# Second half's down products behind the first half's in-projection, and its taps on VectorE

## The reference

```python
# first block, feed-forward
h = rms_norm(x, norm_ffn_g)
gp = dwconv_centered(h @ w_ffn_gate, ffn_conv_w, ffn_conv_b)     # 3 taps along S, 2816 channels
x = x + (silu(gp) * (h @ w_ffn_up)) @ w_ffn_down
# second block, conformer mixer
h = rms_norm_2(x, mix_norm)
a, g = jnp.split(h @ w_in + b_in, 2, axis=-1)
h = a * jax.nn.sigmoid(g)
h = conv(h, conv_w)            # depthwise along S, 31 taps, causal: position s sees s-30 to s
h = silu(layer_norm(h + conv_b, ln_g, ln_b))
x = x + (h @ w_out + b_out)
# second block, MLP
x = x + jnp.square(relu(rms_norm_2(x, mlp_norm) @ w1)) @ w2
```

## Time and profile before

| | |
|---|---|
| median of 3 runs | 3266.32 us (3264.25 to 3274.74) |
| profiled execution | 3276.46 us, its span 3274.6 us |
| mean granted clock of TensorE | 0.982 of full |
| feed-forward, first to last product | about 1454 to 2176 us |
| from there to the first up product | 2176 to 2516.7 us |
| bytes moved | 288.8 MB |

### The profile page before, as it was taken

The page is one execution under the profiler, slowest core; times in us unless marked ns, Lnnn a source line. Parts: engine busy times, 40 slices in busy tenths (PEclk is TensorE's granted clock), DMA queues, the critical chain, the costliest instruction groups (busy, mean ns, idle before and its releaser), DMA issues.

```text
span 3274.6 us, 54823 instructions
## 1 busy us (share of the span) xinstructions
PE 3152.3 (96%) x23414; PEld 2544.0 (78%) x23414; DVE 2012.7 (61%) x3047; ACT 1067.3 (33%) x1528; POOL 374.1 (11%) x354
## 2 busy tenths in 40 slices
PE   8998998899999998999999999999999999999999
PEld 7787886777777777778888888887746888788887
DVE  6665554466766775545444444469979988755544
ACT  5222334445444443222111111132253333433332
POOL 0222441000000000301000000020000000110000
PEclk9999999799999999999999999999999999999999
DMA  3343665122222223421111111111101222223222
GB/s 148 126 135 99 214 213 186 54 75 81 69 86 75 82 81 116 148 90 52 39 52 52 52 42 49 52 39 52 39 13 52 103 91 103 90 90 126 94 91 76
DMA packets 93537, 288.80 MB, mean 88 GB/s; under 512 B 12400, under 2 KB 38640, under 8 KB 72816
## 3 DMA queue, kind: packets, MB, share of 16 engines
q1 hardware_dynamic: 79104, 233.39, 21.1%
q0 software_dynamic: 14192, 51.91, 4.6%
HBM read 228.64 MB, written 56.62 MB: 87 GB/s over the span
## 4 chain that ended last, share of the span: by engine, by line
PE 82%; DVE 10%; ACT 2%; issue 2%; DMA 2%; POOL 1%; SPq 1%; DVEq 0%; ACTq 0%; POOLq 0%
PE ps L2441 24%; PE ps L307 21%; PE ps L489 7%; PE ps L1744 4%; PE ps L2247 3%; PE ps L2603 2%; PE ps L1755 2%; DVE Yh L2630 2%; PE ps L1767 2%; PE ps L2063 1%; PE ps L1387 1%; PE ps L1404 1%; PE ps L1008 1%; PE ps L1398 1%; DVE wlo L287 1%
## 5 line engine op out<-in xcount | busy, mean ns | idle before, releaser
L2441 PE MATMUL ps<-Hh,whi 128*128 128x512 f32 x1600 | 497.6, 392 | 1.3 <-DVE uA L2562 0.7
L283 ACT ACTIVATE whi<-raw 128x2048 fp32r<-128x2048 f32 x139 | 265.5, 1910 | 522.2 <-PE ps L307 296.1
L287 DVE TENSOR_TENSOR wlo<-raw,whi 128x2048 fp32r<-128x2048 f32 x139 | 321.2, 2311 | 95.0 <-ACT whi L283 94.6
L2441 PEld LDWEIGHTS ps<-Hh,whi 128*128 128x128 f32 x1600 | 300.0, 188 | 70.5 <-issue 5.3
L2441 PE MATMUL ps<-Hh,wlo 128*128 128x512 f32 x800 | 311.4, 389 | 0.0
L307 PE MATMUL ps<-Hhi,wlo 128*128 128x512 f32 x672 | 206.9, 389 | 0.0
L307 PE MATMUL ps<-Hlo,whi 128*128 128x512 f32 x672 | 206.9, 389 | 0.0
L307 PE MATMUL ps<-Hhi,whi 128*128 128x512 f32 x672 | 206.8, 389 | 0.0
L2441 PE MATMUL ps<-aHh,whi 128*128 128x512 f32 x512 | 199.5, 390 | 2.7 <-DVE wlo L287 2.5
L2441 PE MATMUL ps<-aLh,whi 128*128 128x512 f32 x512 | 199.2, 389 | 0.0
L2441 PE MATMUL ps<-aHh,wlo 128*128 128x512 f32 x512 | 199.2, 389 | 0.0
(11 more groups left out here) (389 smaller groups left out, 6181.8 us busy)
## 6 DMA issues: line engine op xcount, KB each, us to landing
raw<-in_panels SPq DMA_DIRECT2D x139, 1024.0 KB, 4.8
rwf<-F POOLq DMA_DIRECT2D x16, 1280.0 KB, 6.6
L<-rwf SPq DMA_DIRECT2D x16, 1024.0 KB, 5.0
L<-rwf SPq DMA_DIRECT2D x64, 256.0 KB, 3.5
gts<-so POOLq DMA_DIRECT2D x16, 512.0 KB, 3.5
gl<-gts SPq DMA_DIRECT2D x32, 256.0 KB, 3.6
rwt<-so POOLq DMA_DIRECT2D x15, 512.0 KB, 2.9
qkd<-XTs POOLq DMA_DIRECT2D x16, 384.0 KB, 4.0
```

What stands on the lines that cost most here:

```text
L283: e.activation(whi[i % 2][:, :], raw_of(i)[:, :], AF.Copy).then_inc(*a_hi.up(i))
L287: e.tensor_tensor(wlo[i % 2][:, :], raw_of(i)[:, :], whi[i % 2][:, :].bitcast(F32), OP.subtract).then_inc(*v_lo.up(i))
L2441: m = e.matmul(ap, W[wi][:, kc, n0:n0 + 128], mov[mi][:, kc, :], start=x == 0 and q == 0, stop=x == len(kcs) - 1 and q == 2)
```

## The change

**Down products.** In the feed-forward only the first half's down products stay (48 a block instead of 96, 8 evictions instead of 16). `aH` and `aL` hold 512 positions. The second half's hidden values are split into `aX` and `aY` and stored to DRAM, 2 x 512 KB a block, by POOL's queue (`hid_pool`). Later `rest_pe` multiplies them in three groups of 8, 8 and 6 tiles of hidden channels with 4 panels each (`fe0` to `fe11`), between the first half's in-projection and the second half's; VectorE adds each group's 8 tiles to `xT` (`rest_dve`, 24 evictions).

**Panels split ahead.** The 8 panels of the in-projection and the 12 of `rest_pe` are loaded in the feed-forward by POOL's queue, one per channel, split by ScalarE and VectorE in two pieces each, and stored to DRAM (`save_load`, `save_act`, `save_dve`, `save_store`). In the late part SP's queue loads high and low parts, 2 x 1 MB, into one of three pairs of buffers (`pre_sp`), the in-projection's panels once for each half (28 loads), and the hidden values in groups of 4, 4 and 3 MB (`hb_sp`). Whole panels have two `raw` buffers in the feed-forward instead of three.

**Taps.** All 31 taps of the first half go to VectorE (`on_pe(0, ch)` is 0), taken two channels at a time so that two chains alternate, in portions (`ahead_dve`) between the gating, the evictions of `rest_dve` and the second half's gating. `MORE` is gone. The second half keeps 5 taps a channel on TensorE; their place moves behind the first half's output product.

```diff
     def raw_of(i):
-        return raw[i % 2 if i < WO else i % 3]
+        return raw[i % 2 if i < WO else i % 3 if i < FA else i % 2 if i < CO else 2 if i < CO + 2 else (i - CO - 2) % 3]
...
+    def save_load(e, i):
+        if i == 0:
+            e.wait_ge(*v_lo.by(FA - 2))
+        else:
+            e.wait_ge(*d_ss.by("save", i - 1, 1, "lo"))
+        for s in range(2):
+            e.dma_start(sraw[s][:, :], A["panels"][PIX[SAVED[i]]][:, 1024 * s:1024 * s + 1024]).then_inc(*d_sl.up("save", i, s))
...
+    def save_store(e, i):
+        for s in range(2):
+            cols = slice(1024 * s, 1024 * s + 1024)
+            e.wait_ge(*v_ff.by("save", i, s))
+            e.dma_start(sph[i][:, cols], shi[s][:, :].bitcast(F32)).then_inc(*d_ss.up("save", i, s, "hi"))
+            e.dma_start(spl[i][:, cols], slo[s][:, :].bitcast(F32)).then_inc(*d_ss.up("save", i, s, "lo"))
...
     def ffn_pool(e):
         e.wait_ge(*v_h.by(1, "rs"))
+        save_load(e, 0)
         for ch in range(22):
             e.wait_ge(*a_ff.by("silu", ch))
             e.tensor_tensor(cv, cv, rs2, OP.mult).then_inc(*g_ff.up(ch))
+            if ch and ch % 2 == 0:
+                hid_pool(e, ch // 2 - 1)
+            if ch < len(SAVED):
+                save_store(e, ch)
+            if ch + 1 < len(SAVED):
+                save_load(e, ch + 1)
+        hid_pool(e, 10)
...
+    def pre_sp(e, j):
...
+        else:
+            e.wait_ge(*t_e.by(*PRE[j - 3]))
+        i = j if j < 20 else j - 20
+        e.wait_ge(*d_ss.by("save", i, 1, "lo"))
+        for m, (name, src) in enumerate((("hi", sph), ("lo", spl))):
+            e.dma_start(PW_[j % 3][m][:, :].bitcast(F32), src[i]).then_inc(*d_pre.up("pre", j, name))
...
     def on_pe(h, ch):
-        return MORE.get(ch, NPE) if h == 0 else NPE
+        return NPE if h else 0
...
     def late_pe(e):
         first_pe(e, 0)
+        for ch in range(2, 8):
+            in_pe(e, 0, ch)
+        for g in range(3):
+            rest_pe(e, g)
         first_pe(e, 1)
-        taps_pe(e, 0, 0)
-        for ch in range(2, 8):
-            in_pe(e, ch)
-            taps_pe(e, 0, ch - 1)
-        taps_pe(e, 0, 7)
+        for ch in range(2, 6):
+            in_pe(e, 1, ch)
+        mean_pe(e, 0)
+        in_pe(e, 1, 6)
+        var_pe(e, 0)
+        in_pe(e, 1, 7)
         taps_pe(e, 1, 0)
-        mean_pe(e, 0)
-        taps_pe(e, 1, 1)
-        taps_pe(e, 1, 2)
-        var_pe(e, 0)
-        for ch in range(3, 6):
+        co_pe(e, 0)
+        for ch in range(3, 5):
             taps_pe(e, 1, ch)
-        co_pe(e, 0)
-        taps_pe(e, 1, 6)
         last_pe(e, 0)
-        taps_pe(e, 1, 7)
+        for ch in range(5, 8):
+            taps_pe(e, 1, ch)
...
+        for ch in range(2, 8):
+            ahead_dve(e, 10)
+            in_dve(e, 0, ch)
+        for g in range(3):
+            for n in range(8):
+                ahead_dve(e, 4 if g == 2 else 6)
+                rest_dve(e, g, n)
+                if g == 2 and n:
+                    first_lo_dve(e, 1, range(n - 1, n))
```

More of the change, by code:

```diff
@@ L2303, in down_pe @@
-        last_use[p] = (t, ("x", b, 7, 1))
-    def down_dve(e, p, t, v, b):
+            ap, waits = ring.take(("down", b, n), (v_ff, "x", b, n))
+            for w in waits:
+                e.wait_ge(*w)
+            for kc in range(2):
+                for q, (wi, mi) in enumerate(THREE):
+                    m = e.matmul(ap, W[wi][:, kc, 128 * n:128 * n + 128], (aH, aL)[mi][b % 2][:, kc, :],
+                                 start=kc == 0 and q == 0, stop=kc == 1 and q == 2)
+            m.then_inc(*t_ff.up("x", b, n))
@@ L2306, in down_dve @@
+        last_use[p] = (t_ff, ("x", b, 7))
+    def down_dve(e, b):
         for n in range(8):
-            for h in range(2):
-                e.wait_ge(*t.by("x", b, n, h))
-                e.tensor_tensor(xT[:, n, hs(h)], ring.bank("down", p, n, h), xT[:, n, hs(h)],
-                                OP.add).then_inc(*v.up("x", b, n, h))
+            e.wait_ge(*t_ff.by("x", b, n))
+            e.tensor_tensor(xT[:, n, hs(0)], ring.bank("down", b, n), xT[:, n, hs(0)], OP.add).then_inc(*v_ff.up("x", b, n))
@@ L2518, in first_pe @@
             e.wait_ge(*w)
[L2519 removed]
+        outs = outs_pe(e, [((x, h, 0), (v_e, x, h, 0), W, n0) for x, n0 in (("a", 0), ("gate", 128))])
         for kc in range(8):
@@ new lines, in glu_dve, with in_act @@
+    def glu_dve(e, h, ch):
+        u = u_of(h, ch)[:, 30:542]
+        e.wait_ge(*a_e.by("sg", h, ch))
+        e.wait_ge(*v_e.by("a", h, ch))
+        e.scalar_tensor_tensor(out=u, in0=u, scalar=vec("a_b_in", ch), in1=sgt[ch % 2], op0=OP.add,
+                               op1=OP.mult).then_inc(*v_e.up("u", h, ch))
+    def in_act(e, h, ch):
+        e.wait_ge(*v_e.by("gate", h, ch))
+        e.activation(sgt[ch % 2], sgt[ch % 2], AF.Sigmoid, bias=vec("a_b_in", 8 + ch)).then_inc(*a_e.up("sg", h, ch))
@@ new lines, in edge_dve, with rest_pe @@
+    def edge_dve(e, ch):
+        e.wait_ge(*v_e.by("taps", 0, ch))
+        e.tensor_copy(uB[ch][:, 0:30], uA[ch][:, 512:542]).then_inc(*v_e.up("tail", ch))
+    def rest_pe(e, g):
+        for m_ in range(4):
+            W = pre_pe(e, 8 + 4 * g + m_)
+            if m_ == 0:
+                e.wait_ge(*d_hb.by("hb", g, "hi"))
+                e.wait_ge(*d_hb.by("hb", g, "lo"))
+            for k in range(2):
+                n = 2 * m_ + k
+                half_pe(e, ("x1", g, n), (v_e, "x1", g, n), W, 128 * k, hb[g], range((8, 8, 6)[g]))
@@ L2662, in sub_dve, with sub_act @@
             e.tensor_tensor(Yh[h][:, ch, :], Yh[h][:, ch, :], rsh[h], OP.subtract).then_inc(*v_e.up("Y", h, ch))
-    def sub_act(e, h):
-        for ch in range(8):
+    def sub_act(e, h, chs=range(8)):
+        for ch in chs:
             e.wait_ge(*v_e.by("Y", h, ch))
@@ L2847, in late_dve @@
     def late_dve(e):
-        done["B"] = 0
+        done["A"] = done["B"] = 0
+        for w in (d_hid.by("hid", 10, "lo"), d_ss.by("save", len(SAVED) - 1, 1, "lo")):
+            e.wait_ge(*w)
         for i, u in enumerate(uA):
@@ L2988, in late_act @@
             last_act(e, 0, n + 1)
+            if n == 0:
+                y_act(e, 1, 1)
+                taps_act(e, 1, 3)
+            if n == 2:
+                taps_act(e, 1, 4)
+            if n == 4:
+                y_act(e, 1, 2)
+                taps_act(e, 1, 5)
+            if n == 6:
+                taps_act(e, 1, 6)
         co_panel(panel_act, e, 0, 3)
         root_act(e, ("sum3", 0), 0)
-        y_act(e, 1, 6)
-        y_act(e, 1, 7)
+        for ch in range(3, 7):
+            y_act(e, 1, ch)
+        taps_act(e, 1, 7)
         for kc in range(8):
             scaled_act(e, 0, kc)
+        y_act(e, 1, 7)
         for b in range(16):
@@ L3034, in late_sp @@
     def late_sp(e):
-        panels_sp(e, UIX["mg0"] + 7, UIX["mu4'"])
+        panels_sp(e, UIX["mg0"] + 7, CO)
+        for j in range(3):
+            pre_sp(e, j)
+        hb_sp(e, 0)
+        for j in range(3, 28):
+            pre_sp(e, j)
+            if j in (10, 14):
+                hb_sp(e, j // 4 - 1)
+            if j == 24:
+                panel_sp(e, CO)
+        panels_sp(e, CO + 1, UIX["mu4'"])
         for n in range(8):
@@ L3218, in lay_out @@
         pan(f"fd{b}", fd[256 * b:256 * (b + 1)])
+    for g in range(3):
+        for m in range(4):
+            pan(f"fe{4 * g + m}", fd[1024 * g:min(1024 * (g + 1), 2816), 256 * m:256 * (m + 1)])
     ai, ao = np.asarray(a_w_in_2)[0], np.asarray(a_w_out_2)[0]
```

337 lines of the change are left out of this document (185 added, 152 removed).

## The result

The changed kernel takes **3210.4 us** (median of 4 runs, 3207.2 to 3213.7) against 3266.6 us for the kernel before on the same chip (3264.3 to 3274.7): a ratio of 0.982, 95% interval 0.980 to 0.984. That is 56 us less, where 62 were forecast (3204 us, range 3195 to 3236). Run again beside the experiments it took 3207.9 us against 3267.2, 59 us less, ratio 0.981 (0.980 to 0.983).

The account below looks back on a forecast made before the run. TensorE, busy 96% of the span, was taken to bound the kernel. The terms -54.6 - 7.0 - 4 + 3.2 gave -62.4, say -62 us, from the median 3266.3 to 3204 us, range 3195 to 3236.

Parts of the forecast that it names:

- Products moved (0): 528 second-half down products leave the feed-forward and return as three groups: 119.7 us out, 119.7 us in, zero net.
- Taps (-54.6): Convolution's first half: all 62 taps (124 records) leave TensorE for VectorE, -54.6 us.
- VectorE in time for the mean (0): Second half: VectorE's last 22 taps done at 279.7 us, TensorE wants the last channel at 280.0: 0 us.
- Rival 3: Taps bound the second half; TensorE waits at the mean, 3 us at 0.78 a tap (3207); no separate chance.
- The shared port (0): Group 2: POOL's adds cost VectorE some 0.7 us an output tile, yet its last low part is in time: nothing.
- The end of the wait (-7.0): First up projection: tap groups cover VectorE's scaled input, removing the 4.24 us wait and 2.8 of slow clock.
- The other small waits of the conformer: Waits for squares, one diagonal and the gate were to go: -4 us of the 5.0 left.
- The 1.2 us for diagonals: New wait: last channel's diagonals stand behind a tap group's output on ScalarE, +1.2 us; the variance's squares another +1.
- Feed-forward, prefetch, two raw buffers (0): Extra feed-forward work, POOL's stores, SP's panel loads and two raw buffers all hide behind TensorE: 0 us each.
- U: The end of a channel's up product on TensorE; feed-forward stores were forecast to land at about U + 14.5.
- rival 1: Prefetch or feed-forward stores somewhat late: one gives 3215 us, both 3227; range 3213 to 3230, chance 0.22.
- The 13 more taps end 2.7 us before POOL's sum is wanted (+1): Up and down stage (MLP): 13 more taps left there end in its 13th block, a new wait of +1 us.

## Why the prediction was right, and where a term was off

*Products moved (0).* Right. The feed-forward is 119.9 us shorter, where 528 products make 119.7, and at 100% in the new place.

*Taps (-54.6).* Right: 53.5 to 54.8 us in profiles when they are put back as dummies, 50.4 on medians.

*VectorE in time for the mean (0).* Right to a few tenths, though "without any room". Its last 22 taps, and TensorE's wait for them:

```profile
2312.34 14.66 DVE L2736 SCALAR_TENSOR_TENSOR Yh<-uT,vc,Yh 128x512 f32<-128x512 f32 x22
```

```profile
PE ps L2586 <- DVE Yh L2736: 0.2, 1, 0.2
```

They end at 2327.0, 279.9 us behind the feed-forward's last product; 279.7 was worked out. Counting two queues against each other step by step, each with durations from the trace, was exact enough over 280 us to tell "just in time" from "late". Rival 3 falls with it.

*The shared port (0).* Right that it costs nothing, but too small in size, and the row behind it was misread. Four taps of which one meets one of POOL's additions, and that one alone:

```profile
2241.58 3.77 DVE L2736 SCALAR_TENSOR_TENSOR Yh<-uT,vc,Yh 128x512 f32<-128x512 f32 x4
```

```profile
2242.24 1.77 DVE L2736 SCALAR_TENSOR_TENSOR Yh<-uT,vc,Yh 128x512 f32<-128x512 f32 x1
```

```profile
2241.80 1.67 POOL L2570 TENSOR_TENSOR sgt<-sgt,uT 128x512 f32<-128x512 f32 x1 [3.28 <-ACT uT L2595]
```

Three of the four taps take their usual 0.74 us. The second takes 1.77: it ends 0.55 us behind POOL's addition, so most of its work comes after that. The addition in turn takes 1.67 us instead of 1.30, and the tap that was running when it began ended some 0.5 us into it. So VectorE loses 1.0 us an addition, not 0.7. The Trainium skill ("SBUF — State Buffer", section "SBUF: two separate sides") calls the port an exclusive lock held for a whole instruction. The trace agrees: one instruction runs and the other waits for it, less 0.2 to 0.3 us in which they overlap (1.04 us lost to an addition of 1.30). The eight subtractions of the MLP's 13th block say the same, with POOL's squares beside them:

```profile
2724.80 2.50 DVE L2765 TENSOR_TENSOR Yh<-Yh,rsh 128x512 f32<-128x512 f32 x4
```

```profile
2728.53 11.75 POOL L2570 TENSOR_TENSOR sgt<-sgt,uT 128x512 f32<-128x512 f32 x6
```

Four take 2.50 us, the other four 1.70 us each from start to start, alternating with POOL's operations, which also come every 1.70 us. That makes the 9.32 us above. The prediction's rows show this too, if they are lined up by time. Of the seven subtractions there (2794.05 to 2801.66) the first four lost nothing. The other three met three operations of POOL, the first of them this one, of another form:

```profile
2796.18 1.52 POOL L2464 TENSOR_TENSOR sgt<-uB,uB 128x512 f32<-128x512 f32 x1 [22.92 <-ACT uB L2669]
```

The 3.3 us lost are therefore 1.1 for each of three. The prediction takes the seven as beside six and comes to 0.7. With 1.04 us for each of POOL's seven additions its own count gives some 217.3 us for the last low part, just past the 217.1 at which TensorE wants it. It was there at 2263.0, which is 216.0 us, and no wait came. So the count was over 1 us too long somewhere else, and that the term stayed at 0 is luck in part.

*The end of the wait (-7.0).* Right, and shown by taking the cover away. The clock's 2.8 us in it is this wait's own; another of 8.5 us cost 1.4. The other small waits of the conformer were 6.1 us in all, 1.1 more than the 5.0 of which the prediction took 4 away, and are 2.5 now: 1.2 for diagonals, 0.8 for the bank of the sums, 0.3 for squares, 0.2 for taps. The 1.2 us for diagonals came as forecast; the squares cost 0.3 and not 1. So the conformer is 397.7 us and not 401: -3 us.

*Feed-forward, prefetch, two raw buffers (0).* Right. The stores had landed at 1746.1, U + 14.2 (14.5 was worked out), the slack is 5.0 us (5.2), no product of the in-projection waits for a landing, and rival 1 did not occur. The issues of the page (KB each, us to landing) show both loads of a saved panel well inside the 21.8 us that it is asked for ahead:

```profile
whi<-sph SPq DMA_DIRECT2D x28, 1024.0 KB, 4.9
wlo<-spl SPq DMA_DIRECT2D x28, 1024.0 KB, 7.2
```

***The 13 more taps end 2.7 us before POOL's sum is wanted (+1).* This is the term that was mis-sized.** They end 2.4 us behind it, POOL 4.0. The wait is 4.0 us, and the clock behind it takes 1.4 us in the first profile and 1.7 in the second: 5.4 to 5.7 us where 1 was forecast. I had placed the taps by their number in each block against TensorE's pace. The rows show VectorE without a gap from 2710.6 to 2721.6, one tap behind each eviction, with a panel's split (2.28 us at 2713.11) ahead of the last four taps. The split is about what the taps are late by, so I take it to be what the count left out; no run moved it alone. In the two profiles the MLP is 7.1 and 5.3 us above 757.9 - 2.8. Beside the wait for POOL and its clock that is a new wait of 0.4 us for a split in the third block and, in the first profile, 1.7 us of clock behind the old wait for the split. Taking the taps away gave 3.4 us back, since the old wait then grew to its 2.5 us again and the clock fell behind it.

So the total (-56 and -59 against -62) is close in part because two misses cancel: the conformer came out 3 us better, the MLP 5 to 7 us worse where 1 was priced.

Rival 3 has the clock fall past some 4 us of waiting. That bound doesn't hold: in the kernel before it was at 0.50 for 3.4 us behind a wait of 1.9 us too, at 2843.
